# Values' products with V as the stationary side, two heads side by side, in two of three attention kinds

## The reference, cut to what matters

```python
def block_attention(q, k, v, bias_fn, scale):
    ...
    def one(blk):
        ...
        sc = jnp.einsum('bhqd,bhkd->bhqk', qb, k).astype(jnp.float32) * scale
        p = jax.nn.softmax(sc + bias_fn(qi, ki), axis=-1).astype(v.dtype)
        return jnp.einsum('bhqk,bhkd->bhqd', p, v)
...
o_fox = fox_group(...)    # 4 heads, v has 64 features; mask: key <= query
o_diff = diff_group(...)  # 4 heads, v has 128 features; two softmaxes a head
o_mla = mla_group(...)    # 4 heads, v has 64 features
x = x + jnp.concatenate([o_fox, o_diff, o_mla], axis=-1) @ w_o[i]
```

## Time and profile before

| | us |
|---|---|
| median of 3 runs | 2642.71 |
| lowest, highest | 2642.2, 2642.84 |
| the profiled execution, its own time | 2641.86 |
| its span (first to last instruction) | 2640.4 |
| first attention stage, from the first scores to the end of the output product's first half, of it | 1429.90 to 1602.30 |
| its first kind up to the product at step 10 | 28.9 |
| steps 3 to 7 of the third kind | 17.3 |
| leftover of the third kind and groups 0, 1 | 6.2 |

### The profile page before, as it was taken

How to read it: one execution, slowest core, us unless ns; L and a number is a source line. 1 busy time by engine, 2 the same in 40 slices (tenths; PEclk the granted TensorE clock), 3 DMA queues, 4 the chain that set the end, 5 groups by cost and what they waited for, 6 DMA issues and landing times.

```text
span 2640.4 us, 32796 instructions
## 1 busy us (share of the span) xinstructions
PE 2567.4 (97%) x13272; PEld 1783.5 (68%) x13276; DVE 1157.4 (44%) x2170; ACT 896.9 (34%) x1715; POOL 354.0 (13%) x162
## 2 busy tenths in 40 slices
PE   8999999999999999999999999999999999999999
PEld 6875444444777444444477688888888767888887
DVE  3543322332686222332265433562554644465264
ACT  4431111111483111111164554442345445443233
POOL 2200000000341000000031011222222001123212
PEclk9999999999999999999999999999999999999999
DMA  6229999999423999999932012323131212223212
GB/s 216 67 92 419 419 420 419 420 419 419 154 96 132 419 419 419 420 419 419 419 128 80 33 64 66 110 86 106 64 116 51 80 49 65 64 96 113 87 63 81
DMA packets 139033, 543.26 MB, mean 206 GB/s; under 512 B 18816, under 2 KB 30336, under 8 KB 89728
## 3 DMA queue, kind: packets, MB, share of 16 engines
q1 hardware_dynamic: 129264, 536.94, 52.1%
q10 hardware_dynamic: 9616, 4.18, 0.6%
HBM read 538.99 MB, written 2.10 MB: 205 GB/s over the span
## 4 chain that ended last, share of the span: by engine, by line
PE 92%; DVE 5%; ACT 2%; issue 1%; POOL 0%; DMA 0%; ACTq 0%; POOLq 0%; DVEq 0%
PE ps L615 24%; PE ps L1413 17%; PE ps L617 15%; PE ps L1435 9%; PE ps L1388 5%; PE ps L637 5%; PE ps L549 3%; PE ps L1450 3%; PE ps L1451 2%; PE ps L2017 2%; PE ps L1986 2%; PE ps L550 1%; PE ps L2008 1%; DVE AT L2202 1%; PE ps L467 1%
## 5 line engine op out<-in xcount | busy, mean ns | idle before, releaser
L615 PE MATMUL ps<-w,w 128*128 128x512 f32 x2976 | 678.9, 390 | 2.6 <-POOL w L279 2.6
L615 PEld LDWEIGHTS ps<-w,w 128*128 128x128 f32 x2976 | 557.9, 188 | 119.6 <-POOL w L279 3.4
L279 POOL TENSOR_TENSOR w<-w,w 128x1024 fp32r<-128x1024 f32 (+2 forms) x136 | 329.9, 2434 | 2153.4 <-ACT w L271 2149.1
L1413 PE MATMUL ps<-w,w 128*64 128x512 f32 x2048 | 451.6, 594 | 1.8 <-issue 1.8
L617 PE MATMUL ps<-w,w 128*128 128x512 f32 (+1 forms) x1872 | 408.1, 379 | 3.2 <-DVE w L535 3.0
L271 ACT ACTIVATE w<-w 128x1024 fp32r<-128x1024 f32 (+2 forms) x260 | 252.8, 999 | 416.3 <-PE ps L617 183.4
L617 PEld LDWEIGHTS ps<-w,w 128*128 128x128 f32 x1872 | 337.9, 188 | 69.8 <-issue 4.7
L279 DVE TENSOR_TENSOR w<-w,w 128x1024 fp32r<-128x1024 f32 (+2 forms) x124 | 202.3, 1638 | 385.3 <-ACT w L271 382.7
L1413 PEld LDWEIGHTS ps<-w,w 128*64 128x64 f32 x2048 | 146.0, 137 | 285.5 <-issue 285.5
L1674 DVE TENSOR_TENSOR X<-ps,X 128x512 f32<-128x512 f32 x256 | 162.4, 682 | 181.7 <-PE ps L1451 180.7
L1435 PE MATMUL ps<-w,w 128*64 128x512 f32 x1024 | 226.8, 595 | 0.8 <-ACT w L1502 0.8
(11 more groups left out here) (252 smaller groups left out, 2283.6 us busy)
## 6 DMA issues: line engine op xcount, KB each, us to landing
w<-in_moe_w_gate SPq DMA_DIRECT2D x128, 1024.0 KB, 16.2
w<-in_moe_w_up SPq DMA_DIRECT2D x128, 1024.0 KB, 18.5
w<-in_moe_w_down SPq DMA_DIRECT2D x128, 1024.0 KB, 15.5
w<-in_w_up SPq DMA_DIRECT2D x40, 1024.0 KB, 5.1
w<-in_w_down SPq DMA_DIRECT2D x20, 1024.0 KB, 5.1
w<-in_w_in SPq DMA_DIRECT2D x16, 1024.0 KB, 5.3
w<-in_ab_w_in SPq DMA_DIRECT2D x10, 1024.0 KB, 5.2
w<-in_c_w_in SPq DMA_DIRECT2D x8, 1024.0 KB, 6.1
```

Source lines behind the costliest of these rows:

```text
L279: up(self.wlo[self.low[s][0]], lane.e.tensor_tensor(lo, raw, hi.bitcast(F32), ALU.subtract))
L615: ins = pe.matmul(bank[:, :], wp[:, k, P * o:P * o + P], ap(k0 + k), start=first, stop=stop)
L1413: ins = pe.matmul(bank[64 * e:64 * e + 64, :], XG[p % 3][:, 4 * u + k, 64 * e:64 * e + 64], w[e][:, k, :], start=(u == 0 and k == 0), stop ...
```

## The change

In the first and third kind three things change.

- DVE multiplies the weights themselves (`PB`) by the reciprocal of their row sum, before they are turned: `vector_scaled`, lag 2, two `tensor_scalar` a step from working memory to working memory. PE's transposes wait for it (signal `scaled`) and no longer for the exponential alone.
- In the values' products V is stationary (64 columns) and the turned weights stream (128 columns). The two heads of a step write to rows 0 to 63 and 64 to 127 of one bank, their matmuls alternating. The result has features in rows. For this the first kind's steps now take two heads at the same block too. The second kind's product is as before.
- Features need no turning in these kinds. First kind: DVE copies the bank to `O` (`tensor_copy`, 128x128), and at step 4 of the third kind ACT and DVE split it from there (`scalar_mla_features`, `vector_mla_features`, two instructions of 512 columns each). Third kind: ACT writes the high part from the bank (`scalar_fox_features`, lag 3, behind that step's exponentials), and DVE subtracts it from the bank for the low part, in the place where it moved the values. `FEATURES_OUT` keeps the second kind's four groups, turned at steps 5 and 6. Groups 0 and 1 aren't turned after the last step any more.

```diff
-    FEATURES_OUT = (6, 7, 4, 5, 2, 3, 0, 1)
+    FEATURES_OUT = (4, 5, 2, 3)
...
-                     lambda j, h=h: VM[:, j, 64 * h:64 * h + 64], 64) for h in range(4) for qc in BLOCKS]
+                     lambda j, h=h: VM[:, j, 64 * h:64 * h + 64], 64)
+                    for two in range(2) for qc in BLOCKS for h in (2 * two, 2 * two + 1)]
...
-            at_step = {2: fv}
-            for n in range(3):
-                at_step[4 + n] = lambda n=n: o_feature(FEATURES_OUT[2 * n:2 * n + 2])
+            at_step = {2: fv, 4: mla_feature}
+            for n in range(2):
+                at_step[5 + n] = lambda n=n: o_feature(FEATURES_OUT[2 * n:2 * n + 2])
...
-                    PE.wait_ge(bsc.free, m + 1)
+                    PE.wait_ge(scaled, (m if m < M_DIFF else m - len(diff_jobs)) + 1)
...
-            for m, (qc, _, _, _, _, vals, dv) in turned_jobs(m, two):
-                n = turn_of(m)
-                PE.wait_ge(bpt.free, n + 1)
-                bank = banks.take(bo)
-                for j in range(qc + 1):
-                    ins = pe.matmul(bank[:, 0:dv], PTB[n % 4][:, P * j:P * j + P], vals(j), start=(j == 0), stop=(j == qc))
-                up(bo.full, ins)
+            bank = banks.take(bo)
+            qc, kind, _, _, _, vals, dv = two[0]
+            PE.wait_ge(bpt.free, turn_of(m + 1) + 1)
+            for j in range(qc + 1):
+                if kind == "diff0":
+                    ins = pe.matmul(bank[:, 0:dv], PTB[turn_of(m) % 4][:, P * j:P * j + P], vals(j), start=(j == 0), stop=(j == qc))
+                else:
+                    for e in range(2):
+                        ins = pe.matmul(bank[64 * e:64 * e + 64, 0:P], two[e][5](j), PTB[turn_of(m + e) % 4][:, P * j:P * j + P],
+                                        start=(j == 0), stop=(j == qc))
+            up(bo.full, ins)
...
-                    PE.wait_ge(bo.free, N_TURNS)
-                    tensor_o_features(FEATURES_OUT[6:])
...
+        def scalar_fox_features(m, two):
+
+            qc, kind, h = two[0][:3]
+            if kind == "fox":
+                S.wait_ge(bo.full, m // 2 + 1)
+                up(fox_hi, act.activation(HTH[:, h // 2, P * qc:P * qc + P], bo.banks[bo.full.base + m // 2][:, 0:P], ACT.Copy))
...
+        def scalar_mla_features():
+            S.wait_ge(bo.free, M_DIFF // 2)
+            for k in (6, 7):
+                up(mla_hi, act.activation(by_chunk(HTH[:, k, :]), mla_values(k), ACT.Copy))
...
-            engine = (2, scalar_turn), (0, scalar_scores), (squares_lag, scalar_squares_of_values)
+            engine = (2, scalar_turn), (0, scalar_scores), (3, scalar_fox_features), (squares_lag, scalar_squares_of_values)
...
+        def vector_scaled(m, two):
+
+            if two[0][1] != "diff0":
+                vector_reciprocals(m)
+                V.wait_ge(rc, m // 2 + 1)
+                n = P * (two[0][0] + 1)
+                for m in (m, m + 1):
+                    up(scaled, dve.tensor_scalar(PB[m % 4][:, 0:n], PB[m % 4][:, 0:n], AT[:, 16 + m % 8:17 + m % 8], None, ALU.mult))
...
+            elif kind == "mla":
+                up(bo.free, dve.tensor_copy(O[:, qc, 768 + 64 * h:768 + 64 * h + P], bank[:, 0:P]))
+            else:
+                V.wait_ge(fox_hi, (m - M_FOX) // 2 + 1)
+                at_qc = slice(P * qc, P * qc + P)
+                up(bo.free, dve.tensor_tensor(HTL[:, h // 2, at_qc], bank[:, 0:P], f32(HTH[:, h // 2, at_qc]), ALU.subtract))
...
-            engine = (2, vector_mixture), (0, vector_scores), (sums_lag, vector_reciprocals), (values_lag, vector_values), (1, vector_share)
+            engine = (2, vector_scaled), (2, vector_mixture), (0, vector_scores), (1, vector_sums), (values_lag, vector_values), (1, vector_share)
```

More of the change, by code:

```diff
@@ L1943, in turn_of, with values_before @@
             return M_DIFF + (m - M_DIFF) // 2 if m < M_FOX else m - len(diff_jobs) // 2
+        def values_before(turn):
+            if turn < M_DIFF:
+                return turn // 2 + 1
+            return turn - M_DIFF // 2 + 1 if turn < turn_of(M_FOX) else (turn + len(diff_jobs) // 2) // 2 + 1
         def turned_jobs(m, two):
@@ L2025, in tensor_o_feature, with nothing @@
             tensor_o_features(ks)
+        def nothing():
+            pass
         def tensor():
@@ L2079, in tensor @@
             PE.wait_ge(ba.free, 31 + 4)
-            third_kind(engine, values_of_fox, tensor_o_feature)
+            third_kind(engine, values_of_fox, nothing, tensor_o_feature)
             def rest(unit):
@@ L2085, in rest @@
                     rest_of_third(engine)
-                    PE.wait_ge(bo.free, N_TURNS)
-                    tensor_o_features(FEATURES_OUT[6:])
                     banks.among = ALL_BANKS
             def ready(n):
-                PE.wait_total(bf.free, mark["o"] + 1 + max(FEATURES_OUT.index(k) for k in ROWS_OUT[:n]))
+                k = ROWS_OUT[n - 1]
+                if k in FEATURES_OUT:
+                    PE.wait_total(bf.free, mark["o"] + 1 + FEATURES_OUT.index(k))
+                elif k > 5:
+                    PE.wait_ge(mla_lo, k - 5)
+                else:
+                    PE.wait_ge(bo.free, N_STEPS - 4 + 4 * k)
             banks.among = SCORE_BANKS
@@ L2113, in scalar_turn, with mla_values, by_chunk @@
                 if turn > 3:
-                    S.wait_ge(bo.full, turn - 3)
+                    S.wait_ge(bo.full, values_before(turn - 4))
                 up(bpt.free, act.activation(PTB[turn % 4][:, 0:n], bank[:, 0:n], ACT.Copy))
+        def scalar_fox_features(m, two):
[3 more added lines that the diff above has]
+                up(fox_hi, act.activation(HTH[:, h // 2, P * qc:P * qc + P], bo.banks[bo.full.base + m // 2][:, 0:P], ACT.Copy))
+        def mla_values(k):
+            return O[:, :, P * k:P * k + P]
+        def by_chunk(a):
+            return a.rearrange("p (c n) -> p c n", c=NT)
+        def scalar_mla_features():
+            S.wait_ge(bo.free, M_DIFF // 2)
+            for k in (6, 7):
+                up(mla_hi, act.activation(by_chunk(HTH[:, k, :]), mla_values(k), ACT.Copy))
         def squares_lag(m):
@@ L2202, in vector_scores, with vector_reciprocals @@
                 up(mx, dve.tensor_reduce(AT[:, m % 8:m % 8 + 1], bank[:, 0:n], AX, ALU.max, negate=True))
-        def vector_reciprocals(m, two):
+        def vector_reciprocals(m):
             V.wait_ge(bsc.free, m + 2)
@@ L2207, in vector_reciprocals, with vector_sums @@
             up(rc, dve.reciprocal(AT[:, 16 + i0:18 + i0], AT[:, 8 + i0:10 + i0]))
+        def vector_sums(m, two):
+            if two[0][1] == "diff0":
+                vector_reciprocals(m)
+        def vector_scaled(m, two):
+            if two[0][1] != "diff0":
+                vector_reciprocals(m)
+                V.wait_ge(rc, m // 2 + 1)
+                n = P * (two[0][0] + 1)
+                for m in (m, m + 1):
+                    up(scaled, dve.tensor_scalar(PB[m % 4][:, 0:n], PB[m % 4][:, 0:n], AT[:, 16 + m % 8:17 + m % 8], None, ALU.mult))
         def vector_share(m, two):
@@ L2235, in vector_values, with vector_mla_features @@
         def vector_values(m, two):
-            for m, (qc, kind, h, _, _, _, dv) in turned_jobs(m, two):
-                bank = bo.next(V)
+            bank = bo.next(V)
+            qc, kind, h, _, _, _, dv = two[0]
+            if kind == "diff0":
                 V.wait_ge(rc, m // 2 + 1)
-                c0 = 256 + P * h if kind == "diff0" else (768 if kind == "mla" else 0) + 64 * h
-                up(bo.free, dve.tensor_scalar(O[:, qc, c0:c0 + dv], bank[:, 0:dv], AT[:, 16 + m % 8:17 + m % 8], None, ALU.mult))
+                up(bo.free, dve.tensor_scalar(O[:, qc, 256 + P * h:256 + P * h + dv], bank[:, 0:dv], AT[:, 16 + m % 8:17 + m % 8],
+                                              None, ALU.mult))
+            elif kind == "mla":
+                up(bo.free, dve.tensor_copy(O[:, qc, 768 + 64 * h:768 + 64 * h + P], bank[:, 0:P]))
+            else:
+                V.wait_ge(fox_hi, (m - M_FOX) // 2 + 1)
+                at_qc = slice(P * qc, P * qc + P)
+                up(bo.free, dve.tensor_tensor(HTL[:, h // 2, at_qc], bank[:, 0:P], f32(HTH[:, h // 2, at_qc]), ALU.subtract))
+        def vector_mla_features():
+            for k in (6, 7):
+                V.wait_ge(mla_hi, k - 5)
+                up(mla_lo, dve.tensor_tensor(by_chunk(HTL[:, k, :]), mla_values(k), by_chunk(f32(HTH[:, k, :])), ALU.subtract))
         def vector_o_features(ks):
```

20 lines of the change are left out of this document (8 added, 12 removed).

## The result

The changed kernel takes 2650.99 us (median of 8 runs, 2648.43 to 2653.8), the kernel before, in 8 runs of its own, 2642.77 (2642.01 to 2644.27). The ratio is 1.003, with a 95% interval of 1.0021 to 1.0039: slower by 8.2 us. The profiled execution of the changed kernel took 2653.64 us, so it lies near the top of the runs.

A forecast was written before the change was run, and what follows sets the result against it. PE, busy 97% of the span, was taken as the bound, with a loop through DVE and ACT replacing it in the third kind. Terms -1.1 + 4.1 - 2.1 + 0.6 = +1.5 us a layer gave 2645.7 us, range 2638.5 to 2653.

The forecast's parts named there:

- The likeliest case: Whole kernel: the forecast of 2645.7 us holds, in a band from 2641 to 2650; chance 56%.
- the second rival: Third kind: clock falls in two or three stretches a layer, one into the product; +2.5 us a layer more, 2650.7; 15%.
- The sign: Whole kernel: slower by more than 0.2% (5.3 us) 0.36, faster by more 0.15, within 0.49.
- Values on PE: Values' products on PE: two 64-column halves side by side cost 0.054 us a record instead of 0.108.
- Going over: PE, runs of values: switching to halves and back costs 0.1 us each way, 0.2 in and out.
- The first rival, no overlap: Values on PE: halves do not overlap, 0.108 us a record; +4.7 us a layer, 2655; chance 12%.
- First kind: First kind of attention steps: four steps take 10.8 us instead of 11.46; -1.1 us a layer.
- Second kind: Second kind of attention steps: same instructions in the same order, so no change.
- The loop: Third kind, steps 3 to 7: closed loop through ACT, DVE and PE takes 21.4 us instead of 17.3; +4.1 a layer.
- The third rival, the loop as no bound: Third kind: PE's list sets steps 3 to 7, 13.8 us; 2629, or 2637 for half of it; together 17%.
- Leftover: Leftover turns and values after the last step: 4.1 us instead of 6.2; -2.1 us a layer.
- The clock: Third kind: one stretch at 1.2 GHz a layer, from PE's idle gaps in the loop; +0.6 us a layer.

The follow-up runs named there:

- one_by_one: Changed kernel with the values' products done head after head instead of alternating; 2654.18 us, ratio 1.004.
- no_scale: Changed kernel without DVE's scaling of the weights, so outputs of the first and third kind are not divided by row sums; 2629.34 us, ratio 0.9952.
- first_alone: Kernel before with the change in the first kind only, the third kind left as before; 2641.83 us, ratio 0.9998.
- third_alone: Kernel before with the change in the third kind only, the first kind left as before; 2651.93 us, ratio 1.0037.
- pe_filled: Changed kernel plus six constant matmuls of 512 columns on PE ahead of the turns at steps 4 to 7 of the third kind; 2646.54 us, ratio 1.0014.
- lows_later: Changed kernel with the third kind's low part on DVE moved to lag 4, behind the scalings; 2642.34 us, ratio 1.0002.
- scaled_first: lows_later with the features' 512-column low parts at steps 4 to 6 also moved behind the scalings; 2632.85 us, ratio 0.9958.
- spread: scaled_first with the second pair of the second kind's features groups turned in the leftover instead of step 6; 2632.54 us, ratio 0.9958.
- spread_fed: spread plus eleven constant matmuls in the first kind's idle gap on PE; 2629.76 us, ratio 0.9952.
- before_fed: Kernel before plus eleven constant matmuls in the first kind's idle gap of 2.46 us on PE; 2641.35 us, ratio 0.9997.

## Why the prediction was right or wrong

The range held the time (2650.99, in 2638.5 to 2653). The likeliest case did not quite: it forecast 2645.7 and ended at 2650. The time is that of the second rival, the clock (2650.7), partly by luck: that rival reckons with 6.2 us of clock in both layers, the traces show 4.2. The sign, slower by 0.3%, had a chance of 0.36 against 0.49 for no difference. By the steps of the text:

- **Values on PE.** 0.054 us a record was taken from two bounds. Measured: from 4 to 16 records 0.37 to 1.02 us, 0.054 for each. Going over was put at 0.2 us in and out; 0.15 is left of each run, and the turns ahead of it take 0.09 more than before (0.75 against 0.66 for six), 0.24 together. The first rival, no overlap, is gone by this and by one_by_one. The Trainium skill's page "TensorE: Matmul & The Clock Gate", section "Single matmul latency", has a drain of some 175 ns, which at both ends of a run would be 0.35 by estimate; this trace doesn't agree, with 0.24.
- **First kind.** 10.8 us for four steps forecast, 10.92 measured; -1.1 us a layer forecast, -1.14 and -1.11 measured. In part this is luck of terms that cancel: the values gave 1.48 us with what is left of going over, the turns cost 0.48 more, the scores in their new pairs 0.20, the stall 0.25. The stall behind scores of 128 columns is there, but about half as long: those turns start 0.37 us behind the mask's row, others 0.12. The idle gap at the kind's start grew from 2.46 to 2.68 us, 0.2 where 0.3 was forecast. no_scale prices all waits for the scaling in this kind at 0.42 us.
- **Second kind.** Nothing forecast, -0.3 us measured in each layer. It is a term of the first kind, whose last values stand behind the product at step 10: 8 records in 0.94 us before, 4 in 0.37 after, and a wait behind them that grows. first_alone has the same gain (97.78 us from that product to step 3 of the third kind, against 98.02), third_alone hasn't (98.07).
- **The loop.** Its steps, from one second exponential to the next, the full clock from pe_filled:

| | forecast | pe_filled | changed kernel, layer 1 |
|---|---|---|---|
| step 3 | 2.8 | 2.77 | 2.76 |
| to step 4 | 5.2 | 5.05 | 5.06 |
| to step 5 | 4.6 | 4.47 | 4.47 |
| to step 6 | 5.5 | 5.80 | 6.99 |
| to the product | 3.25 | 3.41 | 4.14 |
| sum | 21.4 | 21.50 | 23.42 |

The sums of the steps are right to 0.3 us. At step 5 the single terms too agree with the rows above to 0.2 us. The third rival, the loop as no bound, falls with it. Its price was too high besides: PE's own list was put at 13.8 us, but in no_scale PE is busy for 14.39 and the steps take 15.65.

- **Leftover.** 4.1 us forecast, 4.04 measured, with the wait of 1.17 us for the scaling.
- **The clock: the term that was mis-sized.** Put at +0.6 us a layer, one stretch a layer that stays inside the third kind. Measured: 2.76 and 1.42 us. In both layers a stretch reaches into the half product, where every matmul is PE's own and the whole loss counts; in layer 1 another lies in the loop. That is not so in every execution: in layer 2 of third_alone the one stretch lies in the loop alone, and the half product takes 11.02 us. The text had the price for that, 1.7 us for each that reaches the product, and gave it 15%. The gaps on PE were known from the loop's own sum (2.2 us at steps 4 and 5, 1.5 at 6 and 7; measured 1.18 and 1.73, then 0.70 and 1.72), and one of 2.46 us had a low clock behind it in the earlier trace rows. Having found the gap of 1.5 us right ahead of the product, it should have been priced there.

With these, the touched stages should have given 3.0 + 3.0 (clock, 4.2 instead of 1.2) - 0.5 (second kind) = 5.5 us, which is what the two traces show. The medians are 8.2 apart. The rest, some 2.7 us, lies outside the touched stages or in how often and how long the clock is at 1.2 GHz: the three runs of the changed kernel with the highest mean clock (0.994) are 5.7 to 6.9 us above the median before, close to what the stages give. pe_filled, first_alone, lows_later, scaled_first and spread each have a first kind with a stretch twice as long in at least one layer (29.2 to 29.3 instead of 27.75 us), and third_alone has one with an unchanged first kind (30.48 instead of 28.87). One profile a kernel does not tell how often. Whether the change makes such stretches more frequent outside its stages stays open.

What the prediction missed beside its number: it wrote down a closed loop with the low part in it, and did not ask where in DVE's queue that low part had to stand. With it and the features' own moved behind the scalings, PE waits for only 1.1 us in steps 3 to 7 (0.45, 0.50 and 0.20 in scaled_first), and the same change is worth 10 us.

## What to carry to other kernels

When work moves from the bound engine to its helpers, write out the loop through all queues that the new waits close, and look for an instruction in it that nobody needs soon: such an instruction, waiting in front of one that the bound engine waits for, is the cost, not the work itself. Moving all of that kind matters; moving one of two gave back only part (2642.3, then 2632.9). A loop that leaves TensorE idle is to be priced with the clock too, at the place that comes behind the gap, and above all where that is pure TensorE work.

## What the runs showed of the hardware

- Two halves of 64 columns overlap at a stream of only 128 columns: 0.054 us a record of float32, 0.24 us for going over and back (0.09 of it in the run ahead). In short runs (8 records) it makes no difference whether the halves alternate (0.60 against 0.59 us); with 16 it does (1.51 against 1.02).
- A low granted clock followed idle gaps of 1.7 to 2.7 us and went away when the gap was filled with constant matmuls (0.94 to 1.00 in the first kind, 0.90 and 0.97 to 1.00 in the third). A gap alone doesn't settle it: lows_later has gaps of 1.17, 1.73 and 0.90 us in layer 1 with no low stretch behind them (clock 1.00), and in layer 2 a low stretch behind the same gap of 1.73 us (clock 0.92 in steps 3 to 7). The gap of 2.68 us in the first kind had 3.4 us at 1.2 GHz behind it in some traces and 6.8 in others.
- Filling idle time with work that nobody needs made a kernel faster: 4.45 us in pe_filled, 2.8 in spread_fed. In before_fed the stages became 3.3 us shorter, but the median did not fall clear of noise.
